# Differential attention in a decoder trunk: the last two heads woven into each other and into the output projection

## What is computed

```python
def _diff_attention(x, wqkv, wo, lam, subln_g, cos, sin, lambda_init):
    q, k, v = jnp.split(x @ wqkv, 3, axis=-1)
    q = _partial_rope(q.reshape(B, S, N_HEADS, 2, HEAD_DIM), cos, sin)      # 8 heads, two maps of 64 each
    k = _partial_rope(k.reshape(B, S, N_HEADS, 2, HEAD_DIM), cos, sin)
    v = v.reshape(B, S, N_HEADS, 2 * HEAD_DIM)
    ...
        p = jax.nn.softmax(jnp.where(causal, s, -1e30), axis=-1)
        a = p[:, :, 0] - lam_full * p[:, :, 1]
        return jnp.einsum('bhqk,bkhe->bqhe', a.astype(v.dtype), v)
    ...
    o = _rms_norm(o, subln_g) * (1.0 - lambda_init)
    return o.reshape(B, S, N_HEADS * 2 * HEAD_DIM) @ wo
...
x = _layer_norm(ALPHA * x + h, ln1_g[i], ln1_b[i])
x = _layer_norm(ALPHA * x + _swiglu(x, ffn_w13[i], ffn_w2[i]), ln2_g[i], ln2_b[i])
```

## Time and profile before

| What | Value |
|---|---|
| Median of 3 runs | 2359.86 us (2354.95 to 2360.16) |
| The profiled execution, its own time | 2357.53 us |
| Its span | 2355.7 us |
| PE busy | 2227.9 us, 95% of the span |
| DVE, ACT, POOL busy | 45%, 30%, 3% |
| Mean granted clock of PE | 0.976 of 2.4 GHz |
| Chain that ended last | PE 75%, issue 22% |
| DMA | 203.40 MB, 86 GB/s in the mean |

### The profile page before, as it was taken

The page is one execution under the profiler, slowest core; times in us unless marked ns, Lnnn a source line. Parts: engine busy times, 40 slices in busy tenths (PEclk is TensorE's granted clock), DMA queues, the critical chain, the costliest instruction groups (busy, mean ns, idle before and its releaser), DMA issues.

```text
span 2355.7 us, 29361 instructions
## 1 busy us (share of the span) xinstructions
PE 2227.9 (95%) x10792; PEld 1837.6 (78%) x10792; DVE 1064.5 (45%) x1498; ACT 715.5 (30%) x1208; POOL 80.4 (3%) x98
## 2 busy tenths in 40 slices
PE   6998799999999889999999799999999979999998
PEld 5766588888888878888888688878886648888787
DVE  2576352223369976322334422233637745222334
ACT  2344332223232413222222322222324433222222
POOL 0000000000030002000000000000000000000000
PEclk9999799999999999999999899999999979999999
DMA  5211133332333005333332233323331103333231
GB/s 186 65 45 45 47 106 106 90 101 95 98 108 99 19 19 153 107 89 101 95 98 63 72 107 89 98 98 98 98 90 46 53 27 90 107 89 106 91 97 63
DMA packets 256390, 203.40 MB, mean 86 GB/s; under 512 B 6224, under 2 KB 235600, under 8 KB 256320
## 3 DMA queue, kind: packets, MB, share of 16 engines
q1 hardware_dynamic: 252688, 189.42, 26.7%
q0 software_dynamic: 3632, 13.02, 1.8%
HBM read 200.32 MB, written 2.10 MB: 86 GB/s over the span
## 4 chain that ended last, share of the span: by engine, by line
PE 75%; issue 22%; DVE 1%; ACT 1%; POOL 0%; DMA 0%; POOLq 0%; ACTq 0%; DVEq 0%
PE ps L1039 23%; PE ps L1040 23%; PE ps L1041 23%; PE ps L1343 3%; PE ps L1108 1%; DVE x_nat L766 1%; PE ps L1410 1%; ACT xT_hi L468 0%; PE ps L1119 0%; PE ps L1331 0%; PE ps L1364 0%; DMA raw<-in_w 0%; PE ps L1124 0%; DVE x_nat L750 0%; ACT prob L658 0%
## 5 line engine op out<-in xcount | busy, mean ns | idle before, releaser
L1039 PE MATMUL ps<-xT_hi,w_hi 128*128 128x512 f32 (+1 forms) x1752 | 678.3, 387 | 0.7
L1041 PE MATMUL ps<-xT_hi,w_lo 128*128 128x512 f32 (+1 forms) x1752 | 673.6, 385 | 0.0
L1040 PE MATMUL ps<-xT_lo,w_hi 128*128 128x512 f32 (+1 forms) x1752 | 673.3, 384 | 0.0
L705 DVE TENSOR_TENSOR w_lo<-raw,w_hi 128x1024 fp32r<-128x1024 f32 x338 | 414.3, 1249 | 362.3 <-ACT w_hi L455 361.8
L455 ACT ACTIVATE w_hi<-raw 128x1024 fp32r<-128x1024 f32 x338 | 355.8, 1058 | 696.6 <-PE ps L1041 693.0
L1041 PEld LDWEIGHTS ps<-xT_hi,w_lo 128*128 128x128 f32 x1752 | 329.2, 188 | 65.8
L1039 PEld LDWEIGHTS ps<-xT_hi,w_hi 128*128 128x128 f32 x1752 | 329.2, 188 | 65.2 <-issue 1.7
L1040 PEld LDWEIGHTS ps<-xT_lo,w_hi 128*128 128x128 f32 x1752 | 329.4, 188 | 63.1
L1024 DVE TENSOR_TENSOR hid<-gate,ps 128x512 f32 (+1 forms) x88 | 60.5, 687 | 673.9 <-PE ps L1041 673.9
L1039 PE MATMUL ps<-w_hi,a_hi 128*128 128x512 f32 x832 | 327.2, 393 | 10.8 <-ACT a_hi L458 10.8
L1041 PE MATMUL ps<-w_hi,a_lo 128*128 128x512 f32 x832 | 325.7, 391 | 0.0
(11 more groups left out here) (123 smaller groups left out, 1814.9 us busy)
## 6 DMA issues: line engine op xcount, KB each, us to landing
raw<-in_w SPq DMA_DIRECT2D x264, 512.0 KB, 4.0
raw<-in_wqkv SPq DMA_DIRECT2D x48, 512.0 KB, 3.8
raw<-in_pw SPq DMA_DIRECT2D x24, 512.0 KB, 4.0
raw<-in_wo SPq DMA_DIRECT2D x16, 512.0 KB, 3.5
ln_gb<-in_g POOLq DMA_DIRECT2D x8, 512.0 KB, 4.2
ln_gb<-in_b POOLq DMA_DIRECT2D x8, 512.0 KB, 5.8
x_nat<-in_x SPq DMA_DIRECT2D x4, 512.0 KB, 6.1
out<-x_nat SPq DMA_DIRECT2D x4, 512.0 KB, 2.6
```

Of the source, the lines that this page charges most:

```text
L705: nc.vector.tensor_tensor(weight_lo(u), raw[:, r, :], weight_hi(u).bitcast(f32), ALU.subtract).then_inc(w_lo_done, 1)
L1039: nc.tensor.matmul(dst, lhs[0], rhs[0], start=start, stop=False, skip_group_check=check)
L1040: nc.tensor.matmul(dst, lhs[0], rhs[1], start=False, stop=False, skip_group_check=check)
L1041: return nc.tensor.matmul(dst, lhs[1], rhs[0], start=False, stop=stop, skip_group_check=check)
```

## The change

The last two heads (y = 6, z = 7) are no longer two calls of `step`: their pieces are written out by hand on PE, ACT and DVE. Scores of the second chunk come before the difference of the first is turned, and the first scores of head 7 before the last values of head 6. Head 7's output goes to bank 0, the turns to bank 3, the scores to banks 4 to 7. The first four chunks of the projection are cut into 16 parts, `part(c, t)`, of which ten stand between the pieces of head 7, and the other six behind them. Their operands are split earlier, each activation chunk when its own head is copied. The last four chunks are as before (`down_end`). The core of the diff (ACT and DVE have their orders written out in the same way as PE):

```diff
-    O_BANK, S_BANK, T_BANK = 2, 3, 7
+    T_BANK, S_BANK = 3, 4
+    def o_bank(j):
+        return 0 if j == HEADS - 1 else 2
...
 ACT
-                step(HEADS - 2)
-                step(HEADS - 1)
-                square(HEADS - 1, None)
-                out_head(HEADS - 1, None)
+                def chunk(c):
+                    act.wait_ge(oT_done, H0 + c + 1)
+                    if c >= RING:
+                        act.wait_ge(w_used, w0 + c - RING + 1)
+                    split_a(hid[:, oT0 + c * SEQ:oT0 + (c + 1) * SEQ], c % RING)
+
+                square(y - 1, None)
+                exps(y, 0, None)
+                exps(y, 1, None)
+                split_w(w0 + 1)
+                turned(y, 0, None)
+                chunk(0)
...
+                for c in range(RING, KD):
+                    split_w(w0 + c)
+                    chunk(c)
                 heads += HEADS
-                def arrived(c, it):
-                    act.wait_ge(oT_done, H0 + HEADS)
-                down(i, "wo", KD, oT0, arrived)
...
 PE
+                def part(c, t, last=False):
+                    chunk_ready(a0 + c + 1)
+                    split_ready(w0 + c)
+                    m = down_block((a_hi[:, c, :], a_lo[:, c, :]), w0 + c, t, c == 0, False)
+                    if last:
+                        m.then_inc(w_used, 1)
...
+                scores(y, 0, None)
+                scores(y, 1, None)
+                unit(2 * z + 1, None, 0)
+                turn_diff(y, 0, None)
+                scores(y, 2, None)
+                turn_diff(y, 1, None)
+                scores(y, 3, None)
+                unit(2 * z + 1, None, 1)
+                turn_head(y - 1, None)
+                values(y, 0, None)
+                turn_diff(y, 2, None)
+                values(y, 1, None)
+                turn_diff(y, 3, None)
+                values(y, 2, None)
+                scores(z, 0, None)
+                scores(z, 1, None)
+                values(y, 3, None)
+                turn_diff(z, 0, None)
+                scores(z, 2, None)
+                turn_diff(z, 1, None)
+                scores(z, 3, None)
+                values(z, 0, None)
+                values(z, 1, None)
+                pe.wait_ge(exp_done, TB * (H0 + z) + 3)
+                part(0, 2)
+                part(1, 2)
+                turn_diff(z, 2, None)
+                pe.wait_ge(exp_done, TB * (H0 + z) + 4)
+                part(0, 3)
+                values(z, 2, None)
+                part(1, 3)
+                part(2, 3)
+                turn_head(y, None)
+                turn_diff(z, 3, None)
+                part(2, 2)
+                values(z, 3, None)
+                pe.wait_ge(oT_done, H0 + HEADS - 1)
+                pe.wait_ge(diffT_done, TB * (H0 + HEADS))
+                part(0, 1)
+                part(3, 2)
+                part(1, 1)
+                turn_head(z, None)
+                part(2, 1)
+                pe.wait_ge(oT_done, H0 + HEADS)
+                part(0, 0, True)
+                part(1, 0, True)
+                part(2, 0, True)
+                part(3, 0)
+                part(3, 1)
+                part(3, 3, True)
...
-                down(i, "wo", KD, lambda: pe.wait_ge(oT_done, H0 + HEADS))
+                down_end(i, "wo", KD)
```

More of the change, by code:

```diff
@@ L604, in square @@
                     for c in range(TB):
-                        e = nc.scalar.activation(gate[:, 0, c * P:(c + 1) * P], ps[:, O_BANK, c * P:(c + 1) * P], ACT.Square,
+                        e = nc.scalar.activation(gate[:, 0, c * P:(c + 1) * P], ps[:, o_bank(j), c * P:(c + 1) * P], ACT.Square,
                                                  accum_out=o_sq[:, c:c + 1])
@@ L612, in out_head @@
                     dst = hid[:, lo:lo + SEQ] if it is None else hid[:, bass.ds(it * (2 * SEQ) + lo, SEQ)]
-                    nc.scalar.activation(dst, ps[:, O_BANK, :], ACT.Copy, scale=gain[:, i // 3:i // 3 + 1]).then_inc(oT_done, 1)
+                    nc.scalar.activation(dst, ps[:, o_bank(j), :], ACT.Copy, scale=gain[:, i // 3:i // 3 + 1]).then_inc(oT_done, 1)
                 def step(j, it=None):
@@ L640, in _ @@
                     step(3, it)
-                step(HEADS - 2)
-                step(HEADS - 1)
-                square(HEADS - 1, None)
-                out_head(HEADS - 1, None)
+                w0, y = unit0[i, "wo"], HEADS - 2
+                z = y + 1
+                def chunk(c):
[9 more added lines that the diff above has]
+                chunk(0)
+                turned(y, 1, None)
+                chunk(1)
+                exps(y, 2, None)
+                chunk(2)
+                exps(y, 3, None)
+                out_head(y - 1, None)
+                split_w(w0 + 2)
+                turned(y, 2, None)
+                split_w(w0 + 3)
+                turned(y, 3, None)
+                chunk(3)
+                exps(z, 0, None)
+                exps(z, 1, None)
+                square(y, None)
+                turned(z, 0, None)
+                turned(z, 1, None)
+                exps(z, 2, None)
+                exps(z, 3, None)
+                turned(z, 2, None)
+                out_head(y, None)
+                turned(z, 3, None)
+                square(z, None)
+                out_head(z, None)
+                for c in range(RING, KD):
+                    split_w(w0 + c)
+                    chunk(c)
                 heads += HEADS
-                def arrived(c, it):
-                    act.wait_ge(oT_done, H0 + HEADS)
-                down(i, "wo", KD, oT0, arrived)
                 blocks(i, 0)
@@ L849, in norm_head @@
                     dve.wait_ge(o_rstd_done, at(it, 1, H0 + j + 1))
-                    nc.vector.tensor_tensor(o_nat[:, :, :], ps[:, O_BANK, :].rearrange("p (t n) -> p t n", t=TB),
+                    nc.vector.tensor_tensor(o_nat[:, :, :], ps[:, o_bank(j), :].rearrange("p (t n) -> p t n", t=TB),
                                             o_rstd[:, :].unsqueeze(2).to_broadcast([P, TB, P]), ALU.mult).then_inc(o_normed, 1)
@@ L906, in _, with chunk @@
                 steps[0] = before + PER * (HEADS // 2 - 2)
[L907 to L910, removed]
+                w0, a0, y = unit0[i, "wo"], chunks_before(i, "wo"), HEADS - 2
+                z = y + 1
+                def chunk(c):
+                    split_a(hid[:, oT0 + c * SEQ:oT0 + (c + 1) * SEQ], c % RING, a0 + c + 1)
+                head_max(y, 0, None)
+                head_max(y, 1, None)
+                mean_square(y - 1, None)
+                combine(y, 0, None)
+                combine(y, 1, None)
+                norm_head(y - 1, None)
+                head_max(y, 2, None)
+                chunk(0)
+                head_max(y, 3, None)
+                combine(y, 2, None)
+                rope_first(2 * z + 1)
+                combine(y, 3, None)
+                rope_second(2 * z + 1)
+                chunk(1)
+                head_max(z, 0, None)
+                head_max(z, 1, None)
+                chunk(2)
+                combine(z, 0, None)
+                combine(z, 1, None)
+                mean_square(y, None)
+                head_max(z, 2, None)
+                split_w(w0 + 1)
+                head_max(z, 3, None)
+                combine(z, 2, None)
+                split_w(w0 + 2)
+                combine(z, 3, None)
+                split_w(w0 + 3)
+                norm_head(y, None)
+                chunk(3)
+                mean_square(z, None)
+                norm_head(z, None)
+                for c in range(RING, KD):
+                    split_w(w0 + c)
+                    chunk(c)
                 heads += HEADS
-                down(i, "wo", KD, oT0)
                 blocks(i, 0, unit0[i, "wo"] + KD - 1)
@@ L1159, in down @@
         def down(i, stage, n, bank_free):
-            half = 1 if stage == "down" else 0
-            u0, a0, b = unit0[i, stage], chunks_before(i, stage), 2 * i + half + 1
-            first_banks = ORDER if stage == "down" and up_bank(i, "up") == 0 else IN_ORDER
+            u0, a0 = unit0[i, stage], chunks_before(i, stage)
+            first_banks = ORDER if up_bank(i, "up") == 0 else IN_ORDER
             def acts(c):
@@ L1183, in down, with down_end, acts @@
                         chunk(c, it)
+            down_end(i, stage, n)
+        def down_end(i, stage, n):
+            half = 1 if stage == "down" else 0
+            u0, a0, b = unit0[i, stage], chunks_before(i, stage), 2 * i + half + 1
+            body = n - TAIL
+            def acts(c):
+                return a_hi[:, c % RING, :], a_lo[:, c % RING, :]
             if to_pooling(b):
@@ L1267, in values @@
                     k = TB * (H0 + j) + c
-                    if c == 0 and H0 + j:
+                    if c == 0 and H0 + j and j < HEADS - 1:
                         pe.wait_ge(oT_done, at(it, 1, H0 + j))
@@ L1273, in values @@
```

(11 more changed lines are left out.)

## The result

The changed kernel takes 2303.14 us (median of 4 runs, 2301.62 to 2303.76), the kernel before 2358.1 us (4 runs, 2354.95 to 2360.16). The ratio is 0.9768, 95% interval 0.9754 to 0.9783. Forecast was 2304 in a range of 2298 to 2314. The profiled spans are 2299.8 and 2355.7 us: 55.9 us less.

The account below looks back on a forecast made before the run. TensorE, 95% busy, loses time at both attention layers' ends: layer 3's 95.7 us becomes 65.8 work + 2.4 waits + 0.8 switching = 69.0. Gains of 26.7 and 27.2 us give 2304 us, range 2298 to 2314.

Parts of the forecast that it names:

- The work that is left: Last two heads 22.3 us at full clock, with the projection 65.8 us of the old 95.7 in layer 3.
- (a): Head 6's first values wait until ScalarE has copied head 5 out of the shared bank: 0.9 us.
- (b): PE's wait ahead of head 7's first turn, while VectorE readies the difference: 1.3 us (0.5 to 1.8).
- (c): Short waits at hand-overs elsewhere in the reordered heads: 0.2 us.
- the switching term: Switching between short and long matmuls at eight places, 0.1 us each: 0.8 us.
- The parts: 16 parts of chunks 0 to 3, moved work, hide waits at head 7's third values, turn and copy.
- The bank: Head 7's output in bank 0 removes the wait of its values for head 6's copy; no size given.
- VectorE's slack: Between head 7's first and third differences VectorE needs 5.5 us while PE does 6.4: slack 0.9, cost 0.
- Rival B: VectorE becomes the bound, PE waits ahead of head 7's third and fourth turn: 2306 to 2310 us, chance 0.2.
- The clock: Half clock costs 12.3 us a layer, 9.7 in the heads and 2.6 on two parts; expected to stay full.
- rival A: The clock falls once in head 7's stretch in both layers: 4 to 6 us a layer, 2312 to 2316, chance 0.12.
- Rivals C and D: C: half clock from projection start onward, 2418 us, chance 0.01. D: parts don't run early, 2357 us, chance 0.02.

Follow-up runs that it names:

- e2: The changed kernel with all 16 parts put behind head 7's turn, heads 6 and 7 still woven and splits still early: 2330.77 us.
- e4: The changed kernel with head 7's output back in bank 2, head 6's bank, and head 6 turned before head 7's first values: 2303.83 us.
- e5: The changed kernel with one more VectorE operation of 1.2 us ahead of head 7's third difference: 2302.22 us.
- e6: The changed kernel with two extra VectorE operations (2.3 us more) ahead of head 7's third difference: 2305.99 us.
- e1: The kernel before, with throwaway matmuls into idle bank 0 in the waits of heads 6 and 7: 2338.91 us against 2359.14.

## Why the prediction was right

**What bounds the kernel.** The local reading held: 55.4 of 55.9 us come from the two stretches.

**The work that is left.** Taken off the 4.7 us behind it, the new stretch is 68.3 us; forecast was 69.0, from 65.8 of work, 2.4 of waits and 0.8 of switching. The waits measured 2.23, and each was the one named: (a) 0.78 for 0.9, (b) 1.22 for 1.3, (c) 0.23 for 0.2. The leftover is 0.3 for 0.8: the switching term was over-sized. The last section has the rows for the part between the pieces, 16.6 us where the prediction's own terms without any switching give 16.8 (nine parts, head 7's values and its last two turns, and two head turns). One work term was a little large as well: the four turns of a head were put at 1.40 and take 1.30 (0.20, 0.32, 0.32 and 0.46 in head 6).

**The parts.** No part waits for its operands, and neither head 7's third and fourth values nor its turn or copy are waited for. e2 shows those waits come back, 9 us of them, and the clock's fall with them, when the parts are taken away.

**The bank.** The prediction says which wait it takes away and gives no price for it: in the woven order it is worth 1.1 us a layer (e4). That has no effect on the sum, since the changed kernel has the bank.

**VectorE's slack.** Laid out at 0.9 us, measured at 0.8 to 1.0 (e5, e6). Rival B, with its chance of 0.2, was near in the sense that two more operations would have made it true.

**The clock.** It stayed at 1.00, so rival A did not happen. The Trainium skill ("TensorE: Matmul & The Clock Gate", "A second HAM failure mode: psum-queue depth-cycling") tells of a kernel in which short idle times between groups made it swing; here waits of 0.8, 0.2 and 1.2 us within 8 us did not, while those of e2, where one of 2.1 us follows that of 1.2, did. The 12.3 us a layer that I put on the clock, as one of two separate terms, is not what the clock alone gives: that is 9.2 (e1), and the waits at full clock are 21.3 in layer 0 and not the 17.2 that were seen. The sum of the two was right, as it came from work left, not from terms added.

**Rivals C and D** have nothing for them in any row: the projection started at full clock and the parts ran early.

**The total.** 27.4 and 28.0 us for 26.7 and 27.2, which is the over-sized switching and a little less waiting. From profiled run to profiled run the kernel went from 2357.53 to 2301.62 us, 55.9 less, where 53.9 was forecast. So the gain was 2 us too small in the forecast, and that 2304 and the measured 2303.14 agree within 1 us is in part luck: the forecast starts from one profiled run, the measured value is a median that lies 1.5 us above its own.

## What to carry to other kernels

Size a reordering by the work that is left plus the waits of the new order, both from start-to-start times at full clock, not by adding up the waits and the slow clock of the old one, which overlap: filled with useless work, the same waits gave back a third of the gain. Chains that alternate between engines at the end of a stage want two things at once: a second chain woven in, and independent matmuls of the next stage cut small enough to be placed in what is left; either alone gave less than half here. Before moving more onto the engine that feeds the woven chains, measure its slack with a throwaway operation: here it was 0.8 to 1.0 us in a stretch of 27.

## What I had not expected of the hardware

A switch from short float32 matmuls to the long ones costs almost nothing where it is repeated closely. Timeline of PE after, layer 3: a third turn without a part behind it, then the pieces of head 7 with the parts between them:

```profile
1868.09 0.49 PE L1345 MATMUL ps<-cst,diff 128*128 128x128 f32 x3
1868.41 0.61 PE L1356 MATMUL ps<-hid,diffT 128*128 128x128 f32 x4
...
1876.93 0.89 PE L1356 MATMUL ps<-hid,diffT 128*128 128x128 f32 x6
...
1880.76 0.49 PE L1345 MATMUL ps<-cst,diff 128*128 128x128 f32 x3
1881.01 0.48 PE L1112 MATMUL ps<-w_hi,a_hi 128*128 128x512 f32 x1
...
1882.48 0.83 PE L1356 MATMUL ps<-hid,diffT 128*128 128x128 f32 x6
1883.07 0.48 PE L1112 MATMUL ps<-w_hi,a_hi 128*128 128x512 f32 x1
...
1885.91 0.60 PE L1363 MATMUL ps<-cst,o_nat 128*128 128x128 f32 x4
...
1893.52 0.48 PE L1112 MATMUL ps<-w_hi,a_hi 128*128 128x512 f32 x1
```

A third turn and one part take 1.72 us from start to start (1880.76 to 1882.48), against the 0.32 (1868.09 to 1868.41) and 1.36 that they take apart; the third values and two parts 3.43 (to 1885.91), less than 0.77 and 2.72. The first long matmul begins 0.25 us after the start of the turns instead of 0.32; it is itself longer. Over all nine parts and what stands between them (1876.93 to 1893.52, 16.59 us) no cost of switching is seen. And throwaway matmuls that compute nothing made the kernel before 20 us faster (e1), by the clock alone.
